# A decoder block on one core: the two gates' sums over partitions as two rounded passes, with their split one unit ahead

## The chip, the core and the metric

One core of a Trainium2 chip runs the whole program. The metric is the device time of one execution in microseconds (us), as the median of several runs. The engines are TensorE (PE, with its weight loads listed apart as PEld), VectorE (DVE), ScalarE (ACT), GpSimd (POOL) and SyncE (SP), which issues most transfers.

## The reference, cut to what matters

```python
cond = jax.nn.silu(c)                                   # c: (1, 2048)
mod = (cond @ w_ada[l] + b_ada[l])[:, None, :]          # w_ada: 2048 x 12288
shift1, scale1, gate1, shift2, scale2, gate2 = jnp.split(mod, N_MOD, axis=-1)
h = rms_norm(x, g_norm1[l]) * (1.0 + scale1) + shift1   # x: 256 x 2048
...                                                     # projections, two attention branches
x = x + gate1 * (merged @ w_out[l])
h2 = rms_norm(x, g_norm2[l]) * (1.0 + scale2) + shift2
x = x + gate2 * (jnp.square(jax.nn.relu(h2 @ w_ff1[l])) @ w_ff2[l])
return rms_norm(x, g_final)
```

All is float32. `gate1` and `gate2` are rows of 2048 numbers, each the product of one vector with a 2048 x 2048 part of `w_ada`.

## The kernel before, in words

The large products run in units. A unit (`token_unit`) is a weight tile of 256 rows by 512 columns times 256 tokens. Each weight tile is loaded into one of five buffers `raw` (SP), rounded by ACT into a tile `whi` (function `hi`, line 701), and the rest is computed by DVE into `wlo` (function `lo`, line 1162). PE then runs twelve matmuls on it (line 1741): for two token tiles and two weight rows, `hi*hi`, `hi*lo` and `lo*hi`. There are 608 units, numbered `g`; ACT and DVE work three units ahead (`LEAD = 3`), and `whi` and `wlo` have four buffers each, so `hi(g + 3)` waits until PE has finished unit `g - 1` (`s_pe`), `lo(g + 3)` waits for `hi(g + 3)`, and unit `g` waits for `lo(g)` (`s_lo`). A `raw` buffer is loaded again once `lo` has read it.

The order on each engine is written out by hand: each engine has the same loops over sections (MIX from unit 192, OUT from unit 320, FF from unit 352), and in each step `u` it first calls `hi` or `lo` for the unit three ahead and then whatever else belongs to that step. At the start of FF the first three steps call no `hi` or `lo`, since those of units 355 to 357 are done within the norm before it (`NORM2_UNITS`).

The vector `mod` is computed beside these units. Its weights come as 8 groups `m` of 16 pieces (`RIDE_AT`); DVE multiplies each piece by a column of `cond` and adds it into `acc`, 128 partitions by 1024 columns (function `ada`, line 1273, counted by `s_ada`). When the 16 pieces are in, the 128 partitions have to be added. This is done by PE at fixed units (`MOD_AT`, function `mod`, ahead of the unit's own matmuls), and DVE copies the result from `ps[7]`. Groups 0 to 3 (shift and scale) are summed into columns at line 1649. Groups 4 to 7 (`m >= GATE1`, the two gates) are summed in two halves `h` of 512 columns at line 1651, with a tile of ones as the stationary operand, so that every partition gets the row; line 1289 copies it into `gate1` or `gate2`. These eight gate sums stand ahead of units 277, 279, 322, 324, 358, 360, 392 and 394. Units 358 and 360 are steps 6 and 8 of FF; unit 322 is step 2 of OUT, in whose step 0 DVE also runs `gated("oa", 3)` (lines 1498 and 1502); in step 40 of FF (unit 392) DVE also runs `residual` (lines 1532 and 1536).

Of the kernel before, what the change touches and what calls it, by code (L numbers as in the profile page):

```python
# [139 lines left out]
def pieces_done(m, k):  # L140

    return 2 * (PIECES + m * KT + k + 1)
# [89 lines left out]
def build(nc, x, c, w_ada, b_ada, g_norm1, w_in, w_gla_a_up, b_gla_a, g_gla_out, b_fox_f,  # L232
# [5 lines left out]
    def region(size):  # L238
        offset[0] += size
        assert offset[0] <= nc.sbuf_usable_end, (offset[0], nc.sbuf_usable_end)  # L240
        return offset[0] - size
# [4 lines left out]
    def new(name, shape, dt=F32):  # L246
        size = 4
        for n in shape[1:]:
            size *= n
        return at(name, shape, region((size + 31) // 32 * 32), dt)  # L250
# [79 lines left out]
    mhi = at("mhi", [P, P], rmask)  # L330
    mlo = at("mlo", [P, P], rmask + P * 4)
    rdiag = at("rdiag", [P, TT, P], rmask)
    acc = new("acc", [P, 2 * NB])
    bi = new("bi", [33, NB])

    gout = at("gout", [P, HV], rm + 4096)
# [73 lines left out]
    s_silu = nc.alloc_semaphore("s_silu")  # L410
    s_ada = nc.alloc_semaphore("s_ada")
    s_modmm = nc.alloc_semaphore("s_modmm")
    s_mod = nc.alloc_semaphore("s_mod")

    s_hi = nc.alloc_semaphore("s_hi")
# [113 lines left out]
    with nc.Block() as block:  # L529
# [127 lines left out]
        def _(act):  # L657
# [33 lines left out]
            def hi(g):  # L691

                if g >= NG:
                    return
                act.wait_ge(s_raw[POS_G[g] % RING], landed(POS_G[g]))
                if g >= NG - WRING:

                    act.wait_ge(s_pe, g - 2 * WRING + 1)
                elif g >= WRING and g < G_LAST:
                    act.wait_ge(s_pe, g - WRING + 1)  # L700
                nc.scalar.activation(parts(g)[0][:], raw[POS_G[g] % RING][:], ACT.Copy).then_inc(s_hi, 1)  # L701
# [246 lines left out]
            for it in range(1, 4):  # L948
                for u in range(24):
# [10 lines left out]
                        fox_heads(3, u)  # L960
                    gla_heads(it, u)

            def gate(what, it):

                if what == "ga":
                    act.wait_ge(s_bk[bank(("ob", it), 0)], emptied(("ob", it)))
                    act.wait_ge(s_bk[bank(("ob", it), 1)], emptied(("ob", it)))
                elif it:
                    act.wait_ge(s_bk[bank(("oa", it - 1), 0)], emptied(("oa", it - 1)))
                    act.wait_ge(s_bk[bank(("oa", it - 1), 1)], emptied(("oa", it - 1)))  # L970
                else:

                    act.wait_ge(s_e, 12)
                take((what, it), tok(gz), ACT.Sigmoid)
# [7 lines left out]
            for it in range(4):  # L982
                for u in range(32):
                    hi(G_MIX + 32 * it + u + LEAD)
                    if u == 0 and not it:
                        gla_stage(4, 0)
                    if u == 8:
                        gate("gb", it)
                    if u == 24:
                        gate("ga", it)  # L990
                    if not it:
                        gla_heads(4, u)
                    if it == 2 and u in (2, 9, 16, 23):

                        act.wait_ge(s_oa, 16)
                        t, half = (u - 2) // 14, (u - 2) // 7 % 2 * (D // 2)
                        act.dma_start(xl[:, t, half:half + D // 2], x_v[:, t, half:half + D // 2]).then_inc(s_xl, 16)
                    if it == 3 and u in (25, 27, 29):
                        for t in range(TT):
                            merged_hi((u - 25) // 2, t)  # L1000
# [15 lines left out]

            for u in range(32):
                hi(G_OUT + u + LEAD)
                if u == 3:
                    for t in range(TT):  # L1020
                        merged_hi(3, t)
                if u == 6:
                    act.wait_ge(s_cvl, 8)
                    act.dma_start(gfin[:], g_final.partition_broadcast(P)).then_inc(s_gfin, 16)
                if u >= 8 and u % 8 == 1:
                    part_squares(1, u // 8 - 1, 2 * (u // 8 - 1), xn[:, 0, 0:NB])
                if u >= 8 and u % 8 == 5:
                    x2_evac(u // 8 - 1)
# [25 lines left out]
            for it in range(4):  # L1054
                for u in range(64):
                    if it or u >= len(NORM2_UNITS):
                        for g in ahead(G_FF + 64 * it + u):
                            hi(g)
                    if u in (8, 16, 24, 32):
                        relu(4 * it + u // 8 - 1)  # L1060
                    if u in (12, 20, 28, 36):
                        ff_hi(4 * it + u // 8 - 1)
                    if it == 3 and u in (41, 49, 57):
                        part_squares(2, u // 8 - 5, 32 + 2 * (u // 8 - 5), junk[:])
# [10 lines left out]
        def _(dve):  # L1075
# [200 lines left out]
            def mod(g):  # L1276

                if g not in MOD_AT:
                    return
                m, h = MOD_AT[g]  # L1280
                dve.wait_ge(s_modmm, mods_before(m) + h + 1)
                if m < GATE1:
                    c0 = (2 + m // 2) * KT + m % 2 * 8
                    flat = modc[:].rearrange("p a k -> p (a k)")
                    i = V.tensor_scalar(flat[:, c0:c0 + 8], ps[7][:, 0:8], 1.0, None, ALU.mult)
                else:
                    dst = gate1 if m < 6 else gate2
                    c0 = (m % 2 * 2 + h) * NB
                    i = V.tensor_scalar(dst[:, c0:c0 + NB], ps[7][:], 1.0, None, ALU.mult)
                i.then_inc(s_mod, 1)  # L1290


            f = slice(32, 32 + FH)

            def small_lo():
# [215 lines left out]
            for it in range(4):  # L1511
                for u in range(32):
                    g = G_MIX + 32 * it + u
                    lo(g + LEAD)
                    mod(g)
                    if u == 0 and it:
                        gated("oa", it - 1)
                    if u == 16:
                        gated("ob", it)
                    if not it:  # L1520
                        gla_heads(4, u)
                    if it == 3 and u in (25, 27, 29):
                        for t in range(TT):
                            merged_lo((u - 25) // 2, t)
                    ada(g)
# [14 lines left out]
            for u in range(32):  # L1540
                g = G_OUT + u
                if u == 31:
                    part_sums(1)
                    residual(("out", 3), gate1, 3, [0])
                lo(g + LEAD)
                mod(g)
                if u == 0:
                    gated("oa", 3)
                if u == 3:
                    for t in range(TT):  # L1550
                        merged_lo(3, t)
                if u in (8, 16, 24):
                    residual(("out", u // 8 - 1), gate1, u // 8 - 1)
                ada(g)
# [43 lines left out]
            for it in range(4):  # L1598
                for u in range(64):
                    g = G_FF + 64 * it + u  # L1600
                    if it or u >= len(NORM2_UNITS):
                        for n in ahead(g):
                            lo(n)
                    mod(g)
                    if u == 0 and it:
                        residual(("down", 4 * it - 1), gate2, 3)
                    if u in (8, 16, 24, 32):
                        ff_sq(4 * it + u // 8 - 1)
                    if u in (12, 20, 28, 36):
                        ff_lo(4 * it + u // 8 - 1)  # L1610
                    if u in (40, 48, 56):
                        residual(("down", 4 * it + u // 8 - 5), gate2, u // 8 - 5)
                    if it == 3 and u in (43, 51, 59):
                        final_gain(u // 8 - 5)
                    ada(g)
# [16 lines left out]
        def _(pe):  # L1632
            T = nc.tensor

            def mod(g):

                if g not in MOD_AT:
                    return
                m, h = MOD_AT[g]
                pe.wait_ge(s_ada, pieces_done(m, KT - 1))  # L1640
                pe.wait_ge(s_mod, mods_before(m) + h)

                if sums_before(g)[1]:
                    pe.wait_ge(s_wadd, sums_before(g)[1])
                if m == 0:
                    pe.wait_ge(s_btd, 4)
                if m < GATE1:
                    for j in range(8):
                        i = T.matmul(ps[7][:, j:j + 1], acc[:, j * P:j * P + P], ones[:, 0:1], start=True, stop=True)  # L1649
                else:  # L1650
                    i = T.matmul(ps[7][:], ones[:], acc[:, h * NB:h * NB + NB], start=True, stop=True)  # L1651
                i.then_inc(s_modmm, 1)

            def shift_sum(g):
# [419 lines left out]
```

## Time and profile before

| | |
|---|---|
| median of 3 runs | 1881.63 us (1879.43 to 1885.69) |
| span of the profiled execution, first to last instruction | 1879.2 us |
| PE busy | 1835.8 us, 98% of the span |
| DVE busy | 1231.8 us, 66% |
| ACT busy | 848.2 us, 45% |
| mean granted TensorE clock | 0.99 of full |
| DMA | 441.5 MB, 235 GB/s |

The span is what the rows count in. No time of its own is given for the profiled execution beside its span, which stands 0.2 us under the fastest of the three runs.

### The profile page before, as it was taken

Reading aid. Unit: us, or ns where it says so; the run is one execution under the profiler, and the core shown is the slowest. Engines: PE = TensorE matmul, PEld = TensorE weight load, DVE = VectorE, ACT = ScalarE, POOL = GpSimd, SP = SyncE. Lnnn points to the kernel's source line nnn. Section 1 sums busy time; section 2 is a strip of 40 time slices with the busy share of each in tenths; the row PEclk is TensorE's granted clock in tenths of the full one; section 3 lists DMA queues with packets and bytes.
Section 4 is the critical chain, followed back from the end, with each engine's and each line's share of the span. In section 5 each row is a group of like instructions: output and inputs, shape, how many; then the busy total and the mean of one; then the engine's idle time right before and its main releaser. Section 6 shows DMA issues by size and latency. Waiting matters only on the chain.

```text
span 1879.2 us, 21671 instructions
## 1 busy us (share of the span) xinstructions
PE 1835.8 (98%) x8351; PEld 1485.1 (79%) x8351; DVE 1231.8 (66%) x1368; ACT 848.2 (45%) x1075; POOL 17.7 (1%) x40
## 2 busy tenths in 40 slices
PE   6998999999999999999999998999999999999998
PEld 3666888888888888888888886888888888888886
DVE  6996666666666667666576777775555555555555
ACT  4444545455544554344444444443444344434443
POOL 1000000000000000000000000000000000000000
PEclk8999999999999999999999998999999999999999
DMA  9998899899997987998899784886666666666663
GB/s 382 399 318 250 215 218 278 240 232 256 206 206 236 214 246 232 250 260 295 276 256 266 254 282 156 286 279 201 192 190 180 194 198 181 190 192 191 188 190 123
DMA packets 214767, 441.50 MB, mean 235 GB/s; under 512 B 18437, under 2 KB 34917, under 8 KB 214282
## 3 DMA queue, kind: packets, MB, share of 16 engines
q1 hardware_dynamic: 213272, 436.57, 78.5%
q10 hardware_dynamic: 1138, 3.50, 0.5%
q8 instruction: 67, 1.10, 0.2%
q14 instruction: 34, 0.28, 0.0%
q0 software_dynamic: 256, 0.05, 0.0%
HBM read 437.92 MB, written 2.10 MB: 234 GB/s over the span
## 4 chain that ended last, share of the span: by engine, by line
PE 89%; DVE 2%; DMA 1%; issue 1%; SPq 1%; ACT 0%; POOL 0%; POOLq 0%; DVEq 0%
PE ps L1741 82%; PE ps L1725 1%; DMA raw<-in_w_in 1%; PE ps L1845 1%; DVE wlo L1162 1%; DVE acch L1134 0%; SPq L592 0%; PE ps L1897 0%; PE ps L1649 0%; PE ps L1651 0%; DVE xT L1567 0%; PE ps L1842 0%; ACT whi L701 0%; PE ps L1854 0%; DVE obT L1571 0%
## 5 line engine op out<-in xcount | busy, mean ns | idle before, releaser
L1162 DVE TENSOR_TENSOR wlo<-raw,whi 128x1024 fp32r<-128x1024 f32 x604 | 738.3, 1224 | 587.4 <-ACT whi L701 585.3
L701 ACT ACTIVATE whi<-raw 128x1024 fp32r<-128x1024 f32 x604 | 639.5, 1060 | 935.9 <-PE ps L1741 719.3
L1741 PE MATMUL ps<-whi,hT 128*128 128x512 f32 x2304 | 742.9, 397 | 5.0 <-DVE wlo L1162 4.6
L1741 PEld LDWEIGHTS ps<-whi,hT 128*128 128x128 f32 x2304 | 435.1, 189 | 114.0 <-DVE wlo L1162 13.1
L1741 PE MATMUL ps<-wlo,hT 128*128 128x512 f32 x1152 | 450.6, 391 | 0.0
L1741 PE MATMUL ps<-whi,obT 128*128 128x512 f32 x1280 | 403.9, 393 | 3.9 <-DVE wlo L1162 2.7
L1741 PE MATMUL ps<-whi,oaT 128*128 128x512 f32 x1248 | 389.0, 390 | 0.0
L1741 PEld LDWEIGHTS ps<-whi,obT 128*128 128x128 f32 x1280 | 242.0, 189 | 56.3 <-DVE wlo L1162 4.2
L1741 PEld LDWEIGHTS ps<-whi,oaT 128*128 128x128 f32 x1248 | 234.3, 188 | 48.9 <-issue 0.5
L1741 PEld LDWEIGHTS ps<-wlo,hT 128*128 128x128 f32 x1152 | 217.7, 189 | 45.4 <-issue 2.2
L1741 PE MATMUL ps<-wlo,obT 128*128 128x512 f32 x640 | 250.5, 391 | 0.0
L1741 PE MATMUL ps<-wlo,oaT 128*128 128x512 f32 x624 | 242.8, 389 | 0.0
L1273 DVE SCALAR_TENSOR_TENSOR acc<-raw,cond,acc 128x1024 f32<-128x1024 f32 x120 | 153.3, 1277 | 0.7 <-DMA raw<-in_w_ada 0.4
L1741 PEld LDWEIGHTS ps<-wlo,obT 128*128 128x128 f32 x640 | 121.1, 189 | 25.1 <-issue 0.5
L1741 PEld LDWEIGHTS ps<-wlo,oaT 128*128 128x128 f32 x624 | 117.2, 188 | 24.6 <-issue 0.5
L1134 DVE SCALAR_TENSOR_TENSOR acch<-first,cond,acch 128x1024 f32<-128x1024 f32 (+1 forms) x60 | 64.1, 1068 | 8.5 <-DMA first<-in_w_ada 5.1
L1532 DVE TENSOR_TENSOR rt<-ps,gate 128x512 f32<-128x512 f32 x40 | 27.4, 684 | 8.4 <-PE ps L1741 8.4
L1699 PE MATMUL ps<-first,cond 128*1 128x512 f32 x48 | 26.9, 660 | 4.1 <-DMA first<-in_w_ada 4.1
L1536 DVE TENSOR_TENSOR xl<-xl,rt 128x512 f32<-128x512 f32 x40 | 27.7, 693 | 4.2
L1580 DVE TENSOR_TENSOR t<-t 128x512 f32<-128x512 f32 x32 | 20.6, 684 | 0.0
L1586 DVE TENSOR_TENSOR oaT<-ps,oaT 128x512 fp32r<-128x512 f32 x32 | 20.5, 682 | 0.0
L1225 DVE SCALAR_TENSOR_TENSOR accv<-raw,modc,accv 128x1024 f32<-128x1024 f32 x15 | 19.1, 1275 | 0.0
(234 smaller groups left out, 783.7 us busy)
## 6 DMA issues: line engine op xcount, KB each, us to landing
raw<-in_w_ff SPq DMA_DIRECT2D x256, 512.0 KB, 4.2
raw<-in_w_in SPq DMA_DIRECT2D x248, 512.0 KB, 6.7
raw<-in_w_ada SPq DMA_DIRECT2D x128, 512.0 KB, 5.2
first<-in_w_ada SPq DMA_DIRECT2D x64, 512.0 KB, 10.2
raw<-in_w_in SPq DMA_DIRECT2D x64, 256.0 KB, 6.1
raw<-in_w_proj_fox SPq DMA_DIRECT2D x32, 512.0 KB, 5.7
raw<-in_w_proj_gla SPq DMA_DIRECT2D x32, 512.0 KB, 5.6
raw<-in_w_out SPq DMA_DIRECT2D x32, 512.0 KB, 5.0
```

What stands on the lines that cost most here:

```text
L701: nc.scalar.activation(parts(g)[0][:], raw[POS_G[g] % RING][:], ACT.Copy).then_inc(s_hi, 1)
L1134: V.scalar_tensor_tensor(b[:, c], a[:, c], cond[:, k:k + 1], bih[:] if k == 0 else b[:, c], ALU.mult, ALU.add).then_inc(s_ada, 2)
L1162: V.tensor_tensor(rest[:], raw[POS_G[g] % RING][:], top[:].bitcast(F32), ALU.subtract).then_inc(s_lo, 1)
L1225: V.scalar_tensor_tensor(acc_, w, col, acc_, ALU.mult, ALU.add).then_inc(s_wacc, inc)
L1273: V.scalar_tensor_tensor(acc[:], raw[pos % RING][:].rearrange("p k n -> p (k n)"), cond[:, k:k + 1], acc[:], ALU.mult, ALU.add).then_inc(s ...
L1532: V.tensor_tensor(rt[:, t, :], ps[bank(name, t)][:], gate[:, cols], ALU.mult).then_inc(s_bk[bank(name, t)], 1)
L1536: V.tensor_tensor(xl[:, t, cols], xl[:, t, cols], rt[:, t, :], ALU.add).then_inc(s_x2, 1)
L1580: V.tensor_tensor(t5[:, t, :], t5[:, t, :], t5[:, t, :], ALU.mult).then_inc(s_act, 1)
L1586: V.tensor_tensor(oaT[:, 4 * b:4 * b + 4, 1, t * P:t * P + P], ps[bank(("up", n), t)][:].rearrange("p (k n) -> p k n", k=4), oaT[:, 4 * b: ...
L1699: T.matmul(ps[6][0:1, :], cond[:, k:k + 1], first[p % FRING][:, 0:NB], start=(p == p0), stop=(p == p1)).then_inc(s_adp, 1)
L1725: i = T.transpose(ps[bank(name, t)][:, k * P:k * P + P], src[:, t, k * P:k * P + P], ident[:])
L1741: i = T.matmul(ps[bank(name, t)][:], src[:, kt, hl, tk], w[:, k, :], start=(kt == 0 and n == 0), stop=(kt == KT - 1 and n == 2))
```

## The change: what it does

For the eight gate sums, a rounded copy of the half of `acc` is made by ACT (`acchi`), the rest is computed by DVE in place (`acclo`, the same memory as `acc`), and PE adds the partitions in two fp32r matmuls, ones times `acchi` and ones times `acclo`, in place of one float32 matmul. ACT's copy and DVE's subtraction stand in the step of the unit before the sum, behind that step's `hi` or `lo`. PE's sum now waits for the subtraction (`s_glo`). The sums of shift and scale stay as they are.

```diff
+    acc_at = region(2 * NB * 4)
+    acc = at("acc", [P, 2 * NB], acc_at)
+    acclo = at("acclo", [P, 2 * NB], acc_at, F32R)
+    acchi = at("acchi", [P, NB], gt + 12288, F32R)
...
+            def gate_hi(g):                                  # ACT
+                m, h = MOD_AT.get(g + 1, (0, 0))
+                if m < GATE1:
+                    return
+                act.wait_ge(s_ada, pieces_done(m, KT - 1))
+                act.wait_ge(s_modmm, mods_before(m) + h)
+                nc.scalar.activation(acchi[:], acc[:, h * NB:h * NB + NB], ACT.Copy).then_inc(s_ghi, 1)
...
                     if it or u >= len(NORM2_UNITS):
                         for g in ahead(G_FF + 64 * it + u):
                             hi(g)
+                    gate_hi(G_FF + 64 * it + u)
...
+            def gate_lo(g):                                  # DVE
+                m, h = MOD_AT.get(g + 1, (0, 0))
+                if m < GATE1:
+                    return
+                n = 2 * (m - GATE1) + h
+                own = slice(h * NB, h * NB + NB)
+                dve.wait_ge(s_ghi, n + 1)
+                V.tensor_tensor(acclo[:, own], acc[:, own], acchi[:].bitcast(F32), ALU.subtract).then_inc(s_glo, 1)
...
                         for n in ahead(g):
                             lo(n)
                     mod(g)
+                    gate_lo(g)
...
                 m, h = MOD_AT[g]                             # PE
-                pe.wait_ge(s_ada, pieces_done(m, KT - 1))
+                if m < GATE1:
+                    pe.wait_ge(s_ada, pieces_done(m, KT - 1))
+                else:
+                    pe.wait_ge(s_glo, 2 * (m - GATE1) + h + 1)
                 pe.wait_ge(s_mod, mods_before(m) + h)
...
-                    i = T.matmul(ps[7][:], ones[:], acc[:, h * NB:h * NB + NB], start=True, stop=True)
+                    T.matmul(ps[7][:], ones[:].bitcast(F32R), acchi[:], start=True, stop=False)
+                    i = T.matmul(ps[7][:], ones[:].bitcast(F32R), acclo[:, h * NB:h * NB + NB], start=False, stop=True)
```

`gate_hi` and `gate_lo` are called in the same way in MIX (behind `hi` and behind `mod`) and in OUT, where `gate_lo` stands ahead of `gated`, `merged_lo` and `residual` of its step.

In the changed kernel the lines are numbered otherwise: 1741 is 1776, 1162 is 1180, 1289 is 1307, 701 is 707.

On DVE at the start of FF, the order before is as follows. The two additions into `acc` are those of units 352 and 354, the four `wlo` rows behind them are units 358 to 361, and the `gate` row copies the sum made at unit 358.

```order
L1273 SCALAR_TENSOR_TENSOR acc<-raw_49,cond,acc 128x1024
L1273 SCALAR_TENSOR_TENSOR acc<-raw_52,cond,acc 128x1024
L1162 TENSOR_TENSOR wlo_60<-raw_53,whi_56 128x1024
L1162 TENSOR_TENSOR wlo_61<-raw_49,whi_57 128x1024
L1162 TENSOR_TENSOR wlo_58<-raw_50,whi_54 128x1024
L1162 TENSOR_TENSOR wlo_59<-raw_51,whi_55 128x1024
L1289 TENSOR_SCALAR gate_86<-ps 128x512
L1162 TENSOR_TENSOR wlo_60<-raw_52,whi_56 128x1024
L1162 TENSOR_TENSOR wlo_61<-raw_53,whi_57 128x1024
L1289 TENSOR_SCALAR gate_86<-ps 128x512
```

The same place on DVE in the changed kernel, from the first `wlo` row (unit 358) on:

```order
L1180 TENSOR_TENSOR wlo_60<-raw_53,whi_56 128x1024
L1180 TENSOR_TENSOR wlo_61<-raw_49,whi_57 128x1024
L1180 TENSOR_TENSOR wlo_58<-raw_50,whi_54 128x1024
L1319 TENSOR_TENSOR acclo<-acc,acchi 128x512
L1180 TENSOR_TENSOR wlo_59<-raw_51,whi_55 128x1024
L1307 TENSOR_SCALAR gate_86<-ps 128x512
L1180 TENSOR_TENSOR wlo_60<-raw_52,whi_56 128x1024
L1319 TENSOR_TENSOR acclo<-acc,acchi 128x512
L1180 TENSOR_TENSOR wlo_61<-raw_53,whi_57 128x1024
L1307 TENSOR_SCALAR gate_86<-ps 128x512
```

The first subtraction stands behind the split of unit 360, and the second behind that of unit 362.

On PE at the same place, the changed kernel has the last matmuls of unit 357, the two passes of the sum, and then the first matmuls of unit 358, whose tiles are `whi_56` and `wlo_60`:

```order
L1776 MATMUL ps<-wlo_59,obT 128x512
L1776 MATMUL ps<-whi_55,obT 128x512
L1685 MATMUL ps<-acchi,ones 128x512
L1686 MATMUL ps<-acclo,ones 128x512
L1776 MATMUL ps<-whi_56,obT 128x512
L1776 MATMUL ps<-wlo_60,obT 128x512
```

Before, one row `L1651 MATMUL ps<-acc,ones 128x512` stands in the place of the two passes; `wlo_60` of unit 358 is the DVE's first row above, two rows ahead of the split of unit 360.

## Rows read from the trace of the kernel before

**Rows 1.** The page, part 4: shares of the chain that ended last, by engine.

```profile
PE 89%; DVE 2%; DMA 1%; issue 1%; SPq 1%; ACT 0%; POOL 0%; POOLq 0%; DVEq 0%
```

**Rows 2.** Windows, whole core: busy time of each engine in each stretch.

```profile
core 0: us, PE busy (x) PEld busy (x) DVE busy (x) ACT busy (x) POOL busy (x), PEclk, DMA share, GB/s
927.00:1139.00 212.00, 212.00 (x958) 174.67 (x957) 148.82 (x146) 91.94 (x106) 0.00 (x0) 1.00 0.86 264
1181.00:1869.00 688.00, 688.00 (x3097) 570.27 (x3096) 401.51 (x401) 294.42 (x321) 0.55 (x1) 1.00 0.65 198
```

**Rows 3.** Timeline at unit 277, PE: start, duration, what, [idle before <-releaser].

```profile
925.35 0.39 PE L1741 MATMUL ps<-whi,hT 128*128 128x512 f32 x1
925.58 1.02 PE L1651 MATMUL ps<-acc,ones 128*128 128x512 f32 x2
...
926.68 0.40 PE L1741 MATMUL ps<-wlo,hT 128*128 128x512 f32 x1
```

**Rows 4.** Timeline, ACT and DVE ahead of that sum: the split of unit 279.

```profile
923.69 1.06 ACT L701 ACTIVATE whi<-raw 128x1024 fp32r<-128x1024 f32 x1 [1.18 <-DMA raw<-in_w_in]
...
924.79 1.23 DVE L1162 TENSOR_TENSOR wlo<-raw,whi 128x1024 fp32r<-128x1024 f32 x1 [1.02 <-ACT whi L701]
```

**Rows 5.** Timeline at the sum ahead of unit 279.

```profile
930.56 1.23 DVE L1162 TENSOR_TENSOR wlo<-raw,whi 128x1024 fp32r<-128x1024 f32 x1 [1.80 <-ACT whi L701]
...
931.93 1.02 PE L1651 MATMUL ps<-acc,ones 128*128 128x512 f32 x2
```

**Rows 6.** Timeline at the sum ahead of unit 322, DVE and PE.

```profile
1051.03 1.28 DVE L1502 TENSOR_TENSOR mtok<-mtok,mt 128x512 f32<-128x512 f32 x2
1052.23 1.22 DVE L1162 TENSOR_TENSOR wlo<-raw,whi 128x1024 fp32r<-128x1024 f32 x1
1052.78 1.02 PE L1651 MATMUL ps<-acc,ones 128*128 128x512 f32 x2
```

**Rows 7.** Timeline at the sum ahead of unit 324.

```profile
1057.75 1.23 DVE L1162 TENSOR_TENSOR wlo<-raw,whi 128x1024 fp32r<-128x1024 f32 x1 [1.80 <-ACT whi L701]
1058.90 1.28 DVE L1506 TENSOR_TENSOR hT<-ps,hT 128x512 fp32r<-128x512 f32 x2
...
1060.02 1.02 PE L1651 MATMUL ps<-acc,ones 128*128 128x512 f32 x2
```

**Rows 8.** Timeline at the start of FF, units 357 to 360.

```profile
1165.52 0.66 PE L1741 MATMUL ps<-whi,obT 128*128 128x512 f32 x1 [1.88 <-DVE wlo L1162]
...
1169.96 1.02 PE L1651 MATMUL ps<-acc,ones 128*128 128x512 f32 x2
1170.72 0.50 PE L1741 MATMUL ps<-whi,obT 128*128 128x512 f32 x1
...
1173.31 3.91 DVE L1162 TENSOR_TENSOR wlo<-raw,whi 128x1024 fp32r<-128x1024 f32 x3 [2.64 <-ACT whi L701]
...
1173.54 1.06 ACT L701 ACTIVATE whi<-raw 128x1024 fp32r<-128x1024 f32 x1 [0.27 <-DMA raw<-in_w_ff]
...
1174.59 0.50 PE L1741 MATMUL ps<-whi,obT 128*128 128x512 f32 x1 [0.86 <-DVE wlo L1162]
...
1174.92 0.40 PE L1741 MATMUL ps<-wlo,obT 128*128 128x512 f32 x1
...
1177.92 1.10 PE L1651 MATMUL ps<-acc,ones 128*128 128x512 f32 x2 [0.30 <-issue]
...
1179.09 0.40 PE L1741 MATMUL ps<-wlo,obT 128*128 128x512 f32 x1
```

**Rows 9.** Windows, after the idle time of 1.88 us; columns as in rows 2.

```profile
1165.70:1169.10 3.40, 3.40 (x9) 2.62 (x10) 3.09 (x5) 1.45 (x2) 0.00 (x0) 0.50 0.00 0
```

**Rows 10.** Timeline at the sum ahead of unit 394, DVE and PE.

```profile
1275.46 1.22 DVE L1162 TENSOR_TENSOR wlo<-raw,whi 128x1024 fp32r<-128x1024 f32 x1
1275.93 1.02 PE L1651 MATMUL ps<-acc,ones 128*128 128x512 f32 x2
```

**Rows 11.** The page, part 5: a DVE two-operand instruction on 512 columns in SBUF.

```profile
L1536 DVE TENSOR_TENSOR xl<-xl,rt 128x512 f32<-128x512 f32 x40 | 27.7, 693 | 4.2
```

More of the change, by code:

```diff
@@ L332, in build @@
     rdiag = at("rdiag", [P, TT, P], rmask)
-    acc = new("acc", [P, 2 * NB])
+    acc_at = region(2 * NB * 4)
+    acc = at("acc", [P, 2 * NB], acc_at)
+    acclo = at("acclo", [P, 2 * NB], acc_at, F32R)
+    acchi = at("acchi", [P, NB], gt + 12288, F32R)
     bi = new("bi", [33, NB])
@@ L412, in build @@
     s_modmm = nc.alloc_semaphore("s_modmm")
+    s_ghi = nc.alloc_semaphore("s_ghi")
+    s_glo = nc.alloc_semaphore("s_glo")
     s_mod = nc.alloc_semaphore("s_mod")
@@ L984, in _ @@
                     hi(G_MIX + 32 * it + u + LEAD)
+                    gate_hi(G_MIX + 32 * it + u)
                     if u == 0 and not it:
@@ L1018, in _ @@
                 hi(G_OUT + u + LEAD)
+                gate_hi(G_OUT + u)
                 if u == 3:
@@ L1546, in _ @@
                 mod(g)
+                gate_lo(g)
                 if u == 0:
@@ L1604, in _ @@
                     mod(g)
+                    gate_lo(g)
                     if u == 0 and it:
```

## The prediction

> **What bounds the kernel now.** I read the page first. The chain that ended last lies on PE for 89% of the span [rows 1]. The windows say it more sharply: between the first gate sum and the end of OUT, PE is busy 212.0 of 212 us, and from the start of FF to its end 688.0 of 688 us, both at the full clock [rows 2]. DVE is busy 149 and 402 us in them. So any time PE waits in there is lost, and any matmul time taken from it is won; nothing later absorbs either. Then I went to the eight gate sums in the timeline, one by one, and read for each what DVE and ACT are doing when PE comes to it, because the change ties PE to DVE there. The units' own matmuls are untouched.
>
> **What the product costs and what two passes cost.** The reader sees in [rows 3] the last matmul of unit 276 at 925.35, the sum at 925.58 (0.23 later, the pitch of the unit matmuls), and the second matmul of unit 277 at 926.68. Taking one pitch off, unit 277 begins at 926.45, so the float32 sum holds PE for 0.87 us. The two new matmuls have the form of the unit's own, fp32r over 512 columns: 2 x 0.23 = 0.46 us. Gain 0.41 us each, 8 x 0.41 = 3.3 us if nothing waits. A unit is twelve pitches, about 2.72 us.
>
> **What the wait costs, in general.** Within one step DVE first splits the unit three ahead, then runs the subtraction. A split of 1024 columns lasts 1.23 us and the next instruction starts 1.15 us after its start (1057.75 to 1058.90 in [rows 7]). The subtraction of 512 columns is not in the trace; the nearest row is an addition of two SBUF operands of that size, 0.69 us [rows 11]. Its bounds are 0.6, half a split, and 0.7. ACT's copy of 512 columns lasts at most the 1.06 us of the copy of 1024 [rows 4]; even so it ends before the split beside it does (1.06 after 1.06 from ACT against 1.15 on DVE), so I cost it at nothing. If it took longer than 1.15, the rest would come on top at each sum. When PE resumes after a wait for DVE, the first matmul starts 0.05 us after DVE's end and the second 0.33 later, where the pitch is 0.23 (split of unit 359 from 1173.31, 1.23 long, then matmuls at 1174.59 and 1174.92) [rows 8]; so I reckon 0.16 us from DVE's end. In short: PE can sum at (start of the split) + 1.15 + 0.69 + 0.16 = start + 2.00.
>
> **The eight sums.**
> 1. Unit 277. The split of unit 279 starts at 924.79; its ACT part had itself waited for a load [rows 4]. PE can sum at 926.79 instead of 925.58: 1.21 us of wait, less 0.41: **+0.80**.
> 2. Unit 279. The split starts at 930.56, as early as PE's progress allows; sum at 932.56 instead of 931.93 [rows 5]: +0.63 - 0.41 = **+0.22**. This is the case with nothing in DVE's way: four buffers let the split begin only when the unit before is done, and split plus subtraction then outlast one unit.
> 3. Unit 322. DVE is busy with `gated` until 1052.23, and only then splits; sum at 1054.23 instead of 1052.78 [rows 6]: +1.45 - 0.41 = **+1.04**.
> 4. Unit 324. PE has transposes in that step, so it arrives late: the sum could start at 1059.75, PE comes at 1060.02 [rows 7]. No wait, **-0.41**. The margin is 0.27 us. The subtraction pushes `merged_lo` back by 0.7 us; what needs it is unit 326, two units later, so that costs nothing; without that cover it would be 0.7.
> 5. Unit 358, the large one. Here PE works with no lead: it reaches the sum at 1169.96, and unit 358 starts at 1170.72. The subtraction stands behind the split of unit **360**. ACT's part of that split waits for its load and runs 1173.54 to 1174.60, DVE follows at 1174.64, the subtraction at 1175.79, and ends at 1176.48 [rows 8]. PE, which today runs unit 358 and most of 359 in this time, stands from 1169.96 until DVE's end at 1176.48, 6.5 us. At the full clock the two passes then hold PE from 1176.64 to 1177.10. Unit 358 ends at 1179.82 and unit 359 follows without a wait, since its split is long done. This replaces the 0.86 us that PE waits for unit 359 today.
> 6. Unit 360. The copy for unit 362 waits for the end of unit 358, so case 2 holds: 0.63 us after the end of unit 359. With unit 358 ending at 1179.82: 359 ends at 1182.54, sum at 1183.17, unit 360 at 1183.63. Today unit 360 starts at 1179.09 - 0.23 = 1178.86 [rows 8]. Sums 5 and 6 together: **+4.77** at the full clock.
>    The clock comes on top. Today PE idles 1.88 us before unit 357, the granted clock is then 0.50 [rows 9], that is 1.2 of 2.4 GHz, and the unit takes 1169.96 - 1165.52 = 4.44 us instead of 2.72 [rows 8]: 1.7 us. An idle time of 6.5 us will not do less; I take the same **+1.7**. From below it is 0 (clock stays), from above twice this, 3.4.
> 7. and 8. Units 392 and 394. The first costs like case 2. At the second DVE comes from `residual` and splits only at 1275.46; sum at 1277.46 instead of 1275.93 [rows 10]. DVE's work there hangs on the end of unit 391, ahead of both sums, so the second wait is fixed against that and swallows the first: 1.53 - 0.41 = **+1.12** for both.
>
> Sum: 0.80 + 0.22 + 1.04 - 0.41 + 4.77 + 1.70 + 1.12 = **+9.2 us**. The profiled execution would go from a span of 1879.2 to 1888.4. The median of the runs shown is 2.4 above that span, so I forecast 1881.6 + 9.2 = **1890.8 us**, 0.5% slower.
>
> Whether DVE could run the subtraction ahead of a split whose input is late decides sum 5. In [rows 8] the three splits run in the order of the program, each when its input is there. The Trainium skill (TensorE: Matmul & The Clock Gate, section "Architectural detail: the array is 16× 32×32, not 1× 128×128") says that ScalarE and VectorE are strict first-in first-out, and that PE alone may pull a weight load forward while matmuls stay in order; the trace agrees. It speaks against the change, which puts a short job that PE needs now behind a long one that PE needs two units later. If the engines did pass over a waiting instruction, sum 5 would be a gain of 0.41 and the total about +3.
>
> **Rivals.**
> - The clock also falls after the shorter waits at sums 1, 3 and 8 (1.2 to 1.5 us). For: the fall at 1.88 us. Against: after 0.86 us of idle time unit 359 went from 1174.59 to the next sum at 1177.92 in 3.3 us, 0.30 of it a wait [rows 8], which leaves no room for half the clock. Each costs up to 1.7: 1892.5 to 1895.9.
> - The wait at sum 5 is short. This needs the load of unit 360 to land 3 us earlier or more. DVE's work ahead of it sets when buffers come free, and the change does not touch it, which is against. If sums 5 and 6 cost only what case 2 costs, 0.44, the total is +3.2, 1884.8: no measurable change.
> - The other side: no wait anywhere. The decision is at 0.63 us per sum, the margin by which split and subtraction outlast a unit; if DVE ran ahead by more than that, all eight would gain, -3.3, 1878.3, still within 0.3%. At four of the eight places the rows show DVE more than 1.2 us late, which is against.
> - The change does not do what it says: each fp32r pass with ones takes what the whole product takes. Then each sum holds PE for 1.74 us in place of 0.46, 10.2 us more than forecast, 1901. Against: the unit matmuls, of that form too, run at 0.23 [rows 3].
>
> **How the numbers follow.** A measurement of this kernel tells about 0.3%, 5.6 us, from no change. Forecast case (1888 to 1893): 0.65. More clock falls: 0.17, slower. Short wait at sum 5: 0.10, same. No wait: 0.04, same, with a sliver that reads as faster. Costlier pass: 0.04, slower. Slower is then 0.86, same 0.12, faster 0.02. The forecast's own bounds: clock term 0 or 3.4 gives 7.5 to 10.9 us; subtraction at 0.6 takes off 0.5; the median itself moves by some 2 us. So 1886.5 below. Above, two of the three further clock falls, 1896.
>
> **What would show it.** In the trace of the changed kernel PE should idle ahead of the sum of unit 358 for about 6.5 us, released by the subtraction on DVE, with the granted clock at 0.50 behind it; and for about 0.6 to 1.5 us at the other sums save that of unit 324. Unit 360 should start some 6.5 us later than its place today, after earlier shifts of about 1.7 us are taken off. The subtraction should last 0.6 to 0.7 us. The prediction is wrong if the idle time at unit 358 is under 3 us, if a later idle time of today shrinks by as much, or if the two passes hold PE for more than 0.5 us.

## The result, and the profile after

The changed kernel takes 1891.89 us, median of 6 runs (1890.11 to 1897.03); the kernel before, run beside it, 1884.41 us (1879.43 to 1885.69, 6 runs). The ratio is 1.0047, 95% interval 1.0032 to 1.0062: 0.5% slower. The profiled execution took 1891.19 us, with a span of 1889.4 where the kernel before had 1879.2. That is 10.2 us between two single executions, where the ratio says 8.9 and the two medians 7.5, so the places below show where the time goes better than how much it is.

The page of the changed kernel, parts 1 and 4. PE is busy 2 us less than before and yet the span is 10.2 us longer, and PE's share of the chain falls from 89% [rows 1] to 86%.

```profile
PE 1833.8 (97%) x8351; PEld 1485.3 (79%) x8351; DVE 1235.9 (65%) x1376; ACT 852.1 (45%) x1083; POOL 17.7 (1%) x40
PE 86%; DVE 3%; DMA 2%; issue 1%; ACT 1%; SPq 1%; POOL 0%; POOLq 0%; DVEq 0%; ACTq 0%
```

The view of waits of the changed kernel, PE, from 900 us on: total, times, longest. The first row is new. Seven of the eight sums wait for the subtraction on DVE, and one of these waits is 8.0 of the 11.6 us. The second row is waits for splits: 2.5 us ahead of unit 357 (1.9 before) and 0.7 at unit 311.

```profile
PE ps L1685 <- DVE acclo L1319: 11.6, 7, 8.0
PE ps L1776 <- DVE wlo L1180: 3.3, 2, 2.5
```

The timeline of the changed kernel at the sums of units 277, 322, 358, 360 and 394. It answers to [rows 3 to 8] and [rows 10].

```profile
923.48 1.06 ACT L707 ACTIVATE whi<-raw 128x1024 fp32r<-128x1024 f32 x1 [0.36 <-PE ps L1776]
...
924.57 1.22 DVE L1180 TENSOR_TENSOR wlo<-raw,whi 128x1024 fp32r<-128x1024 f32 x1 [0.20 <-ACT whi L707]
925.72 0.68 DVE L1319 TENSOR_TENSOR acclo<-acc,acchi 128x512 fp32r<-128x512 f32 x1
...
926.46 0.50 PE L1685 MATMUL ps<-acchi,ones 128*128 128x512 f32 x1 [0.35 <-DVE acclo L1319]
926.79 0.40 PE L1686 MATMUL ps<-acclo,ones 128*128 128x512 f32 x1
...
1053.80 1.22 DVE L1180 TENSOR_TENSOR wlo<-raw,whi 128x1024 fp32r<-128x1024 f32 x1
...
1055.67 0.50 PE L1685 MATMUL ps<-acchi,ones 128*128 128x512 f32 x1 [1.17 <-DVE acclo L1319]
...
1167.65 0.50 PE L1776 MATMUL ps<-whi,obT 128*128 128x512 f32 x1 [2.54 <-DVE wlo L1180]
...
1174.38 1.06 ACT L707 ACTIVATE whi<-raw 128x1024 fp32r<-128x1024 f32 x1 [4.90 <-DMA raw<-in_w_ff]
1175.47 2.56 DVE L1180 TENSOR_TENSOR wlo<-raw,whi 128x1024 fp32r<-128x1024 f32 x2 [2.67 <-ACT whi L707]
1175.72 1.06 ACT L707 ACTIVATE whi<-raw 128x1024 fp32r<-128x1024 f32 x1 [0.28 <-DMA raw<-in_w_ff]
1176.68 0.61 ACT L976 ACTIVATE acchi<-acc 128x512 fp32r<-128x512 f32 x1
...
1177.95 0.68 DVE L1319 TENSOR_TENSOR acclo<-acc,acchi 128x512 fp32r<-128x512 f32 x1
...
1178.69 0.79 PE L1685 MATMUL ps<-acchi,ones 128*128 128x512 f32 x1 [8.03 <-DVE acclo L1319]
1179.28 0.63 PE L1686 MATMUL ps<-acclo,ones 128*128 128x512 f32 x1
...
1184.45 0.39 PE L1776 MATMUL ps<-wlo,obT 128*128 128x512 f32 x1
...
1187.45 0.50 PE L1685 MATMUL ps<-acchi,ones 128*128 128x512 f32 x1 [0.33 <-DVE acclo L1319]
...
1190.99 0.39 PE L1776 MATMUL ps<-wlo,obT 128*128 128x512 f32 x1
...
1284.60 1.22 DVE L1180 TENSOR_TENSOR wlo<-raw,whi 128x1024 fp32r<-128x1024 f32 x1
...
1286.48 0.50 PE L1685 MATMUL ps<-acchi,ones 128*128 128x512 f32 x1 [1.05 <-DVE acclo L1319]
```

At unit 358 the reader sees the whole mechanism. The copies for units 359 and 360 start when their loads land (1174.38, 1175.72). The gate's own copy, 0.61 us long, has to wait until 1176.68. DVE runs two splits from 1175.47 and comes to the subtraction at 1177.95. PE has stood since unit 357 and starts at 1178.69. So two things meet: the loads of units 359 and 360 are late, and the subtraction stands behind both of their splits.

The idle time in brackets is shorter than the delay that a wait causes, because it counts from the end of the last matmul. At unit 277 it is 0.35 us. That matmul ends 0.16 us after the next could have started (a matmul lasts 0.39, the pitch is 0.23), and the second pass follows 0.33 us behind the first, 0.10 more than the pitch. Together this is the 0.6 us of delay that the prediction counts.

Windows of the changed kernel, columns as in [rows 2]: before and behind that wait.

```profile
1166.00:1173.00 7.00, 3.01 (x12) 2.17 (x12) 6.12 (x7) 1.80 (x3) 0.00 (x0) 1.00 0.23 54
1173.24:1183.48 10.24, 4.79 (x11) 3.80 (x12) 4.88 (x5) 3.58 (x4) 0.00 (x0) 0.50 0.99 363
1183.48:1190.00 6.52, 6.19 (x27) 4.76 (x26) 3.52 (x4) 3.61 (x5) 0.00 (x0) 1.00 0.28 84
```

The granted clock is 0.50 from 1173.24 to 1183.48, so for 4.8 us after PE resumed at 1178.69. What this costs can be read off the rows above. From the first pass to the second matmul of the second unit behind it (units 359 and 361) it takes 5.76 us at unit 358 (1178.69 to 1184.45) and 3.54 us at unit 360 (1187.45 to 1190.99, at the full clock): 2.2 us.

To place the loss, I took from both traces the start of the second matmul of each unit and subtracted. The table gives how much later (+) it is in the changed kernel, in us, and beside it the step between two places against the prediction's term.

```
unit     later by   step over the sum(s)   predicted
276      +0.36
277      +0.58      +0.22                  +0.80
279      +0.78      +0.22 (from 0.56)      +0.22
321      +1.57
322      +2.60      +1.03                  +1.04
323      +2.57
324      +2.16      -0.41                  -0.41
357      +2.00
358      +9.07
360      +9.15      +7.15 (from 357)       +6.47
391      +9.14
394      +10.26     +1.12 (both)           +1.12
607      +10.23
```

The six steps make 9.3 us. The other 0.9 come from elsewhere: 0.36 from before unit 276, 0.8 around unit 311, where PE waited 0.7 us for a split in this execution and not in that of before, less some 0.25 in small steps back.

### The profile page after: what moved, and what is told of

Its sections match the earlier page's. It is cut to its first block, busy times and chain, and to the rows that moved or that the text cites. A ratio compares the mean times of both kernels' runs of the same rounds, so it can differ in the third digit from the quotient of the medians.

```text
span 1889.4 us, 21695 instructions
## 1 busy us (share of the span) xinstructions
PE 1833.8 (97%) x8351; PEld 1485.3 (79%) x8351; DVE 1235.9 (65%) x1376; ACT 852.1 (45%) x1083; POOL 17.7 (1%) x40
## 4 chain that ended last, share of the span: by engine, by line
PE 86%; DVE 3%; DMA 2%; issue 1%; ACT 1%; SPq 1%; POOL 0%; POOLq 0%; DVEq 0%; ACTq 0%
PE ps L1776 80%; DMA raw<-in_w_in 2%; PE ps L1760 1%; DVE wlo L1180 1%; ACT whi L707 1%; PE ps L1880 1%; DVE acch L1152 0%; SPq L598 0%; PE ps L1932 0%; PE ps L1683 0%; DVE xT L1597 0%; PE ps L1877 0%; PE ps L1889 0%; DMA raw<-in_w_ff 0%; DVE obT L1601 0%
## 5 line engine op out<-in xcount | busy, mean ns | idle before, releaser
L1776 PEld LDWEIGHTS ps<-whi,hT 128*128 128x128 f32 x2304 | 435.3, 189 | 114.3 <-DVE wlo L1180 13.5
```

The lines of the kernel that those rows point to most:

```text
L1776: i = T.matmul(ps[bank(name, t)][:], src[:, kt, hl, tk], w[:, k, :], start=(kt == 0 and n == 0), stop=(kt == KT - 1 and n == 2))
```

## The experiments

Each was timed against the kernel before, run beside it on the same chip; ratios are to that kernel, with 95% intervals. A comparison with the changed kernel goes by two such ratios, and carries the intervals of both. Where units are said to become later in a trace, the shift is taken as in the table above. The first question was whether the loss is the waits or the passes.

**e1_passes_only: the passes without the split.**

```diff
-                    i = T.matmul(ps[7][:], ones[:], acc[:, h * NB:h * NB + NB], start=True, stop=True)
+                    top, rest = parts(g)
+                    pe.wait_ge(s_lo, g + 1)
+                    T.matmul(ps[7][:], ones[:].bitcast(F32R), top[:, 0, :], start=True, stop=False)
+                    i = T.matmul(ps[7][:], ones[:].bitcast(F32R), rest[:, 0, :], start=False, stop=True)
```

> The kernel before with the eight float32 sums replaced by two fp32r passes over weight tiles that the next unit reads anyway. No split of acc, no wait for one. It leaves the gates' values out (what is summed is not acc). Theory (the waits cost, the passes save): each sum holds PE 0.41 us less, 3.3 us less than the kernel before in all, 0.2%. In the trace every sum's next unit starts 0.4 us sooner relative to the sum. Rival (an fp32r pass with ones is as dear as the whole product): 7 to 10 us slower than before.

Measured: 0.9982 (0.9971 to 0.9993), 12 runs, faster by 0.2%, 3.4 us (1.3 to 5.5). The timeline of this kernel at unit 277, PE: both passes and the unit's own matmuls follow each other 0.22 to 0.23 us apart, where the float32 sum held PE for 0.87 [rows 3].

```profile
925.35 0.39 PE L1744 MATMUL ps<-whi,hT 128*128 128x512 f32 x1
925.57 0.39 PE L1653 MATMUL ps<-whi,ones 128*128 128x512 f32 x1
925.80 0.39 PE L1654 MATMUL ps<-wlo,ones 128*128 128x512 f32 x1
926.03 0.39 PE L1744 MATMUL ps<-whi,hT 128*128 128x512 f32 x1
```

Unit 277 starts 0.42 us sooner than before, and the step is 0.39 to 0.42 at every sum save that of unit 358. There the added wait for `s_lo` makes the sum itself wait for the split of unit 358. So the passes are worth what they were priced at, and the rival of the dear pass falls. That the time gives 3.4 us for 3.3 is closer than its interval can vouch for; the steps in the trace are the sharper evidence.

**e2_wait_only: the split and its wait, without the passes.**

```diff
-                V.tensor_tensor(acclo[:, own], acc[:, own], acchi[:].bitcast(F32), ALU.subtract).then_inc(s_glo, 1)
+                V.tensor_tensor(acc[:, own], acc[:, own], acchi[:].bitcast(F32), ALU.subtract).then_inc(s_glo, 1)
...
-                    T.matmul(ps[7][:], ones[:].bitcast(F32R), acchi[:], start=True, stop=False)
-                    i = T.matmul(ps[7][:], ones[:].bitcast(F32R), acclo[:, h * NB:h * NB + NB], start=False, stop=True)
+                    i = T.matmul(ps[7][:], ones[:], acc[:, h * NB:h * NB + NB], start=True, stop=True)
```

> The changed kernel with its copy on ACT, its subtraction on DVE and PE's wait for it kept, but PE then does one float32 product as before (over what is left in acc, so the gates' values are left out). Theory: slower than the changed kernel by what the passes save, 0.4 us at each of eight sums, 3.3 us, so some 13.5 us slower than before. Waits ahead of the sums of the same length as in the changed kernel. Rival (the waits are small and the new passes are what costs): equal to the kernel before.

Measured: 1.0072 (1.0055 to 1.0089), 13.5 us slower than before (10.4 to 16.8), as the theory had it. In its view of waits the seven waits are those of the changed kernel (total, times, longest):

```profile
PE ps L1684 <- DVE acc L1318: 11.1, 7, 7.9
```

The two halves of the change add up: -0.18% and +0.72% make +0.54%, against +0.47% measured.

**e3_all_but_358 and e4_only_358: one sum undone, and that one alone.** A function `is_split(m, h)` stands in the place of `m >= GATE1` in ACT's copy, DVE's subtraction and PE's sum; the other sums are done as before.

```diff
+def is_split(m, h):
+    return m >= 4 and (m, h) != (6, 0)      # e3;  e4: return (m, h) == (6, 0)
...
-                if m < GATE1:
+                if not is_split(m, h):
                     return
```

> The changed kernel, but the sum ahead of unit 358 alone is done as before (float32, waiting for acc only). Theory (seven tenths of the loss lie in this one wait): 6.5 to 7.5 us faster than the changed kernel, about 3 us slower than before; idle time of PE ahead of unit 358 back to 0.5 us, the granted clock of 0.50 after unit 356 back as before. Rival (the loss is spread over the eight sums): 0.8 to 1.3 us faster than the changed kernel.

> The kernel before, with the sum ahead of unit 358 alone split and done in two passes as in the changed kernel. Theory: 6.5 to 7.5 us slower than before, PE idle 6 to 8 us ahead of unit 358. Rival (loss spread evenly): 1 us slower than before.

Measured: e3 1.0027 (1.0015 to 1.0039), 10 runs, 5.1 us slower than before, so 3.8 us faster than the changed kernel by the two ratios, less than the 6.5 expected. The intervals of e3 and of the changed kernel (from 1.0032) overlap, so e3's time does not rule out the rival's 1.3. e4 1.0033 (1.0019 to 1.0047), 7 runs, 6.2 us slower than before (3.6 to 8.9), where 6.5 to 7.5 were expected and the rival said 1: this one does. The times of these kernels move by 3 to 4 us either way between runs, so the place in the trace is the sharper reading. In e3's trace the units become 1.4 us later from 357 to 360, in place of 7.15. In e4's they become 6.4 us later, and the view of waits of e4 from 927 to 1869 us has one wait for a subtraction:

```profile
PE ps L1697 <- DVE acclo L1329: 8.0, 1, 8.0
```

Two expectations for e3 were wrong. The granted clock stayed at 1.00 around unit 357. And the waits did not go back to those of before. The timeline of e3, PE, at the sums of 358 and 360:

```profile
1176.16 1.12 PE L1695 MATMUL ps<-acc,ones 128*128 128x512 f32 x2 [1.05 <-DVE acc L1301]
...
1186.13 0.50 PE L1697 MATMUL ps<-acchi,ones 128*128 128x512 f32 x1 [1.97 <-DVE acclo L1329]
```

Unit 357 at the full clock brings PE to the float32 sum 1.05 us before the last piece is added into `acc`. The sum of unit 360 now waits 1.97 us in place of 0.33: in the changed kernel the long wait ahead of unit 358 hides this one. So undoing one sum gives back less than its own wait.

**e5_late_sums and e6_late_f32: the third pair of sums two units later, with the split and without.** Is PE's missing lead at unit 358 the cause? Both kernels have this edit; e5 on the changed kernel, e6 on the kernel before.

```diff
-_g = ride(6, _g, 2, G_FF + 6)
+_g = ride(6, _g, 2, G_FF + 8)
```

> The changed kernel with the sums of units 358 and 360 moved to 360 and 362 (and so those of 392 and 394 to 394 and 396); the splits still stand one unit ahead of their sum, behind the units' split. Theory (at 358 the loss comes from PE having no lead there): at 360 the subtraction is ready near 1180.2 in the time of the kernel before, PE comes at 1177.3, so a wait of 3 us is left in place of 8, with no fall of the clock behind it; about 4 us slower than the kernel before, 6 us faster than the changed one. Rival (the split ahead is late by the same amount wherever the sum stands): no faster than the changed kernel.

> The kernel before with the same move of four sums and nothing else, as the control of the run beside it. Theory: the float32 sum at 358 lay for 0.7 us beside PE's wait for the split of unit 358, and loses that cover; 0.6 us slower than before, which no measurement tells from nothing. Rival (the move itself gains several us): 3 us or more faster than before, and then the gain of the late sums is no evidence on the waits.

Measured: e5 1.0038 (1.0026 to 1.0050), 5 runs, 7.2 us slower than before where 4 was expected; e6 1.0007 (0.9996 to 1.0019), 12 runs, no measurable difference. Between e5's interval and that of the changed kernel there is overlap, so the timing alone doesn't show a gain. In e5's trace the sum of the third pair that moved to 360 waits 1.7 us, where the sum at 358 waited 8.0 and 3 was expected, and the units become 5.7 us later from unit 276 to 500, in place of 9.9. That is what a missing lead at unit 358 would give, in one trace. What I had left out is at the fourth pair, which moved along to 394 and 396: there both kernels now meet DVE's `residual`, and e5's longest wait for a subtraction is there, ahead of unit 394, 2.8 us. The timeline of e6 there, DVE and PE:

```profile
1282.20 1.28 DVE L1273 SCALAR_TENSOR_TENSOR acc<-raw,cond,acc 128x1024 f32<-128x1024 f32 x1
...
1283.53 1.12 PE L1651 MATMUL ps<-acc,ones 128*128 128x512 f32 x2 [1.02 <-DVE acc L1273]
```

The last piece of the group is added only behind `residual`, and even the float32 sum, at unit 394, waits 1.0 us for it.

**e7_split_first: ahead of the step's `hi` and `lo` in place of behind them.**

```diff
+                    gate_hi(G_FF + 64 * it + u)
                     if it or u >= len(NORM2_UNITS):
                         for g in ahead(G_FF + 64 * it + u):
                             hi(g)
-                    gate_hi(G_FF + 64 * it + u)
```

and so for `gate_lo` and `lo`, and in MIX and OUT.

> The changed kernel with ACT's copy and DVE's subtraction ahead of the step's hi and lo in place of behind them. Theory (what the subtraction stands behind decides): six of the waits vanish and those sums gain 0.41 us each; ahead of unit 358 the copy still stands behind the split of unit 359, whose load is late as well, so DVE's subtraction ends near 1175.2 where it ended at 1176.5, and PE still idles some 5 us there. About 2.5 us slower than the kernel before, 7 us faster than the changed kernel. Rival (a pass over acc on ACT and DVE delays the units' splits wherever it stands): as slow as the changed kernel.

Measured: 1.0022 (1.0012 to 1.0031), 11 runs, 4.1 us slower than before, about 4.7 faster than the changed kernel (1.0047), where 2.5 and 7 were expected; the intervals just miss each other (1.0031 against 1.0032). The view of waits of e7 from 900 us on:

```profile
PE ps L1685 <- DVE acclo L1319: 8.4, 3, 6.9
```

Three waits are left of seven, and 6.9 us at unit 358: the copy still stands behind that of unit 359, whose load is late too. DVE's subtraction did come 1.1 us sooner after the start of unit 357, near the 1.3 expected. The 5 us that I expected of the wait counted from where PE comes when unit 357 runs at half the clock; here, as in the changed kernel, it ran at the full clock and PE was there sooner. In the trace the units become 6.1 us later from 357 to 360.

**e8_first_late: both edits.**

> Both: copy and subtraction ahead of the step's hi and lo, and the sums of 358 and 360 at 360 and 362. Theory: no wait over 0.7 us is left at any sum; 2.5 us faster than the kernel before, 0.13%, near the 3.3 us of the passes alone. Rival (the copy and the subtraction cost PE time through the units' splits): equal to the kernel before or slower.

Measured: 1.0000 (0.9988 to 1.0011), 11 runs: the loss is gone, but the gain of the passes is not there. The time is what the rival said; only the trace, and the run after this one, speak against it. One wait for a subtraction is left, 2.4 us at unit 394, for the reason seen in e6. The timeline of e8 there, DVE, ACT and PE:

```profile
1272.47 0.69 DVE L1565 TENSOR_TENSOR xl<-xl,rt 128x512 f32<-128x512 f32 x1
1273.08 1.28 DVE L1291 SCALAR_TENSOR_TENSOR acc<-raw,cond,acc 128x1024 f32<-128x1024 f32 x1
1274.39 0.63 ACT L976 ACTIVATE acchi<-acc 128x512 fp32r<-128x512 f32 x1 [5.28 <-DVE acc L1291]
1275.05 0.69 DVE L1319 TENSOR_TENSOR acclo<-acc,acchi 128x512 fp32r<-128x512 f32 x1 [0.70 <-ACT acchi L976]
...
1275.80 0.50 PE L1685 MATMUL ps<-acchi,ones 128*128 128x512 f32 x1 [2.41 <-DVE acclo L1319]
```

**e11_all_in_time: two units ahead, first in the step, and both pairs moved.** On top of e8:

```diff
-_g = ride(7, _g, 2, _g + 2 * KT)
+_g = ride(7, _g, 2, _g + 2 * KT + 2)
...
-                m, h = MOD_AT.get(g + 1, (0, 0))
+                m, h = MOD_AT.get(g + 2, (0, 0))
```

> The changed kernel with the copy and the subtraction two units ahead of their sum and ahead of the step's hi and lo, and the sums of the third and fourth pair at units 360 and 362, and 396 and 398 (two later than in the run before, where DVE's residual stood in the way of unit 394). Theory: no sum waits for a subtraction for more than 0.3 us; 2 to 3.3 us faster than the kernel before, 0.1 to 0.2%, as the passes alone were. Rival (copy and subtraction cost PE time in another way): equal to the kernel before or slower, with new waits for wlo.

Measured: 1878.62 us, ratio 0.9981 (0.9972 to 0.9989), 11 runs: faster than the kernel before by 0.2%, 3.6 us, and faster than the changed kernel by 0.7%. This is the version that beats both. No sum waits for a subtraction. Its timeline at the sum ahead of unit 360:

```profile
1171.91 0.62 ACT L976 ACTIVATE acchi<-acc 128x512 fp32r<-128x512 f32 x1
1173.19 0.68 DVE L1319 TENSOR_TENSOR acclo<-acc,acchi 128x512 fp32r<-128x512 f32 x1
...
1175.26 0.39 PE L1685 MATMUL ps<-acchi,ones 128*128 128x512 f32 x1
...
1175.48 0.39 PE L1686 MATMUL ps<-acclo,ones 128*128 128x512 f32 x1
```

The subtraction ends 1.4 us before PE comes. The copies and the subtractions are all there, and the gain is that of the passes alone (3.4 us in e1), so when they are in time they cost PE nothing that can be measured. Against e8 the run changes two things at once, the two units ahead and the place of the fourth pair; which of them removes the wait at unit 394 was not tested apart.

**e12_busy_wait: what the clock's fall costs.**

```diff
+                pe.wait_ge(s_mod, mods_before(m) + h)
+                if (m, h) == (6, 0):
+                    for j in range(24):
+                        T.matmul(ps[7][:], ones[:].bitcast(F32R), hT[:, j % KT, :, :], start=True, stop=True)
```

> The changed kernel with 24 fp32r matmuls of ones times hT, 5.4 us at the full clock, in PE's order between the end of unit 357 and its wait for the subtraction ahead of unit 358; their result is overwritten. Theory (the clock falls because PE idles there, on top of the wait): the granted clock stays at 1.00 behind the wait, unit 358 starts no later and is over in 2.7 us in place of 4.3, and the kernel is 1.7 to 2.4 us faster than the changed one though it computes more. Rival (the clock's fall costs nothing beyond the wait): as long as the changed kernel, or longer.

The windows of this kernel over the same place:

```profile
1166.00:1173.00 7.00, 6.97 (x31) 5.43 (x29) 4.32 (x4) 1.97 (x3) 0.00 (x0) 1.00 0.71 235
1173.00:1183.00 10.00, 7.22 (x31) 5.67 (x32) 6.02 (x8) 4.82 (x7) 0.00 (x0) 1.00 0.77 274
```

The granted clock stayed at 1.00, though PE still idled 2.4 us ahead of the sum, and from unit 357 to unit 360 this kernel's units become 4.8 us later in place of 7.15. The difference of 2.3 us agrees with the 2.2 us read off the changed kernel's own rows. The timing does not confirm it: 1.0044 (1.0030 to 1.0058), 5 runs, is not to be told from the changed kernel's 1.0047, where 1.7 to 2.4 us less were expected. The profiled execution took 1885.7 us and the median was 1891.4, so the one trace need not stand for all runs.

## Why the prediction was right

The forecast was 1890.8 us, the measured median is 1891.9. A part of this closeness is luck. The kernel before ran at 1884.4 this time, 2.8 us above the base of the forecast, and the change itself cost 7.5 us by the medians and 8.9 by the ratio, for +9.2. Within the sum, two terms were off by about 0.6 us each in opposite directions. The mechanism, a sum that waits on DVE, at unit 358 above all, is what the runs show.

- **PE bounds, nothing absorbs.** Right: the loss of each sum stays in all later units to the end of FF (9.14 at unit 391, 10.23 at 607).
- **The price of the product and of the passes.** Right: the step at unit 324, the one sum without a wait, is -0.41, and e1 gains 3.4 us where 3.3 was reckoned.
- **The general wait, start of the split + 2.00 us.** In the changed kernel the split at unit 394 starts at 1284.60 and PE at 1286.48, the second pass 0.33 later: 1.98 by the same reckoning. The subtraction lasts 0.68 us (0.69 was taken), the copy 0.61 and never limits.
- **Sum 1** was mis-sized: +0.22 for +0.80. The load for unit 279, which was late in the trace of before, was in time here (in the changed kernel the copy was released by PE), so this sum is like sum 2. In e2 and e3 the same step was +0.6 and +0.75: it is a matter of when that load lands in an execution.
- **Sums 2, 3, 4, 7 and 8**: within 0.01 us in this trace.
- **Sums 5 and 6**: +7.15 for +6.47. The term off is the clock. I took 1.7 us, the cost of the fall of before over one unit, and allowed 0 to 3.4; the changed kernel's rows give 2.2, and e12's trace 2.3. The two passes ran at half the clock too, which I had put at the full clock. The idle time was 8.0 us for 6.5, because unit 357 ran at the full clock this time and PE got there earlier; the end of the wait is set by DVE and did not move with it. What counts is when unit 358 starts, and that was set by the subtraction on DVE, behind the splits of units 359 and 360 and their late loads.
- **The order on DVE decides**, weighed against a passing-over of the late split: the subtraction ran behind it, with 8.0 us of wait at unit 358 in the changed kernel and in e4, and when e7 moves the subtraction in the order, the waits follow. The Trainium skill (TensorE: Matmul & The Clock Gate, section "Architectural detail: the array is 16× 32×32, not 1× 128×128") says that ScalarE and VectorE are strict first-in first-out, and these traces agree.
- **The rival of further clock falls** behind the short waits did not come: no fall followed the waits of 0.3 to 1.2 us in the changed kernel.

My expectations for the mended kernels were less good than the prediction: e5 and e8 came out 3.2 and 2.5 us slower than expected, outside their intervals. The step that failed was the same in both, and the control e6 shows it by itself: a moved sum takes the next pair with it, and I did not look at what DVE does at the new places. e7 came out 1.6 us slower than expected, within its interval (2.3 to 5.8 us slower than before).

## What to carry to other kernels

When cheaper work on the bounding engine needs preparation elsewhere, read for each place when the preparing engine gets to it and what stands ahead of it in its order; here some 3.4 us of saving came with some 13.5 us of waiting. Look above all for places where the bounding engine has used up its lead, such as the start of a stage: one of eight sums, with the one behind it, made 7.15 of the 10.2 us in the trace. Put the short job ahead of the long one and further ahead of its use, and check the places that the move shifts as well.

## What the runs showed of the hardware that was not expected

Whether an idle time of PE of about 2 us is followed by a fall of the granted clock differs between executions: 1.88 us ahead of unit 357 was [rows 8, 9], and 2.54 us at the same place in the changed kernel was not. Nor does the length of the idle time decide ahead of unit 358: 2.18 us in e11 was followed by a clock of 0.50 from 1168.26 to 1171.67, and 2.27 us in e1 by none. Behind the 8.0 us the clock stayed low for 4.8 us after PE resumed.
